# A decoder step's head: small loads issued from GpSimd, bias rows emptied by VectorE, x loaded behind the second unit's pages

## What is computed

```python
def compress(rows, w1, b1, w2, b2):            # cached raw K or V rows, blocks of 32 at a stride of 16
    h = b1
    for r in range(CMP_RATIO):
        h = h + jnp.einsum('bngf,fe->bnge', ch[:, r:r + n_cmp], w1[r])
    return jnp.einsum('bnge,ed->bngd', jax.nn.silu(h), w2) + b2
...
    s = s + tbl[t5_bucket(dist_c)].transpose(2, 3, 0, 1)      # relative-position bias on every score
...
def swiglu_half(x, gain, w_gu, w_down):
    g, u = jnp.split(rms_norm(x, gain) @ w_gu, 2, axis=-1)
    return x + 0.5 * ((jax.nn.silu(g) * u) @ w_down)
```

## Time and profile before

| | |
|---|---|
| median of 3 runs | 3188.43 us (3187.55 to 3188.77) |
| the profiled execution | 3181.32 us |
| its span, first to last instruction | 3179.7 us |
| PE busy | 2992.5 us, 94% of the span |
| PE on the chain that ended last | 91% |
| first matmul of the compression | 47.17 us |
| first matmul of the first block | 255.08 us |

### The profile page before, as it was taken

The page is one execution under the profiler, slowest core; times in us unless marked ns, Lnnn a source line. Parts: engine busy times, 40 slices in busy tenths (PEclk is TensorE's granted clock), DMA queues, the critical chain, the costliest instruction groups (busy, mean ns, idle before and its releaser), DMA issues.

```text
span 3179.7 us, 46641 instructions
## 1 busy us (share of the span) xinstructions
PE 2992.5 (94%) x18952; PEld 2815.2 (89%) x18952; DVE 1450.1 (46%) x1776; ACT 974.3 (31%) x1092; POOL 119.9 (4%) x180
## 2 busy tenths in 40 slices
PE   6999999999999999999994767969999999999999
PEld 3788999999999999999983556649999999999999
DVE  2424445334444444565545434354444433444433
ACT  3423332223222333333323111123343322322322
POOL 0000000000000011100000000121000000000000
PEclk9999999999999999999996655569999999999999
DMA  7364554455554555433214440235454445545444
GB/s 186 101 190 121 149 152 146 139 162 157 150 146 137 148 181 204 147 132 113 107 54 130 137 125 20 65 113 153 139 151 145 137 141 158 159 145 152 131 139 139
DMA packets 675398, 437.43 MB, mean 138 GB/s; under 512 B 29133, under 2 KB 664029, under 8 KB 667741
## 3 DMA queue, kind: packets, MB, share of 16 engines
q1 hardware_dynamic: 661026, 421.29, 44.1%
q0 software_dynamic: 1856, 12.87, 1.1%
q10 hardware_dynamic: 12396, 1.61, 0.5%
HBM read 422.33 MB, written 21.65 MB: 140 GB/s over the span
## 4 chain that ended last, share of the span: by engine, by line
PE 91%; SPq 3%; DVE 2%; issue 1%; ACTq 1%; DMA 1%; POOL 1%; ACT 0%; DVEq 0%; POOLq 0%
PE bank L406 21%; PE bank L407 21%; PE bank L408 21%; PE bank L738 4%; PE bank L740 4%; PE bank L739 4%; PE bank L1266 2%; PE bank L666 2%; PE bank L668 2%; PE bank L667 2%; SPq L1344 1%; PE bank L1105 1%; PE bank L1573 1%; PE bank L1567 1%; SPq L1357 1%
## 5 line engine op out<-in xcount | busy, mean ns | idle before, releaser
L406 PE MATMUL bank<-xh,whi 128*128 128x320 f32 x3072 | 951.4, 310 | 20.1 <-POOL xl L1837 20.1
L407 PE MATMUL bank<-xl,whi 128*128 128x320 f32 x3072 | 950.4, 309 | 0.0
L408 PE MATMUL bank<-xh,wlo 128*128 128x320 f32 x3072 | 950.4, 309 | 0.0
L312 DVE TENSOR_TENSOR wlo<-wraw,whi 128x2048 fp32r<-128x2048 f32 (+1 forms) x321 | 649.8, 2025 | 523.6 <-ACT whi L308 522.7
L308 ACT ACTIVATE whi<-wraw 128x2048 fp32r<-128x2048 f32 (+1 forms) x321 | 543.3, 1693 | 716.9 <-PE bank L408 716.9
L406 PEld LDWEIGHTS bank<-xh,whi 128*128 128x128 f32 x3072 | 578.0, 188 | 21.3 <-POOL xl L1837 21.0
L407 PEld LDWEIGHTS bank<-xl,whi 128*128 128x128 f32 x3072 | 578.0, 188 | 0.2 <-issue 0.2
L408 PEld LDWEIGHTS bank<-xh,wlo 128*128 128x128 f32 x3072 | 577.7, 188 | 0.0
L406 PE MATMUL bank<-hh,whi 128*128 128x320 f32 x1408 | 436.2, 310 | 9.2 <-DVE hl L366 9.2
L407 PE MATMUL bank<-hl,whi 128*128 128x320 f32 x1408 | 435.7, 309 | 0.0
L408 PE MATMUL bank<-hh,wlo 128*128 128x320 f32 x1408 | 435.5, 309 | 0.0
(11 more groups left out here) (308 smaller groups left out, 2568.8 us busy)
## 6 DMA issues: line engine op xcount, KB each, us to landing
wraw<-in_w_ffn_gate_up SPq DMA_DIRECT2D x176, 1024.0 KB, 5.4
wraw<-in_w_ffn_down SPq DMA_DIRECT2D x128, 704.0 KB, 4.5
wraw<-in_w_mix SPq DMA_DIRECT2D x52, 1024.0 KB, 4.8
pages<-in_cache_cmp SPq DMA_DIRECT2D x128, 128.0 KB, 2.1
wraw<-in_w_mix_out SPq DMA_DIRECT2D x16, 1024.0 KB, 5.4
kt_s<-in_slc_k SPq DMA_DIRECT2D x64, 128.0 KB, 2.0
s_v<-in_slc_v SPq DMA_DIRECT2D x64, 128.0 KB
o_win_sample<-in_state_win_kv POOLq DMA_DIRECT2D x8, 1008.0 KB, 15.7
```

The lines of the kernel that those rows point to most:

```text
L312: dve.tensor_tensor(wlo[:, a % 2, 0:size], wraw[:, a % RAW, 0:size], whi[:, a % 2, 0:size].bitcast(F32), ALU.subtract).then_inc(s["lo_read ...
L406: pe.matmul(b, whi[:, a % 2, c], h[:, kk, :], start=first, stop=False)
L407: pe.matmul(b, whi[:, a % 2, c], lo_[:, kk, :], start=False, stop=False)
L408: mm = pe.matmul(b, wlo[:, a % 2, c], h[:, kk, :], start=False, stop=end)
```

## The change

POOL issues the 19 small loads, and the bias store behind them. DVE copies the bias rows, out of four banks instead of two. ACT's list begins with onehot, the table and both halves of the first key weights. `onehot` moves to the memory of `kcs`, `vcs` and `xt`, so x is loaded only when the bias rows are done; it is issued behind the second unit's pages, and its tiles are handled in units 2 to 6. ident is issued behind the first unit's pages. The waits for the small loads move to where they are first needed.

```diff
-N_SMALL = 21
+N_SMALL = 19
...
-        onehot = at("onehot", 172.125, [33, C_ALL])
+        onehot = at("onehot", 8.125, [33, C_ALL])
...
-            return range(KT * (u - 1) // 6, KT * u // 6) if 1 <= u <= 6 else range(0)
+            return range(KT * (u - 2) // 5, KT * (u - 1) // 5) if 2 <= u <= 6 else range(0)
...
-            sp.dma_start(ident[:, :], io["c_ident"]).then_inc(s["ld_ident"], 16)
             sp.dma_start(ptab[:, :], ...).then_inc(s["ld_pt"], 16)
-            first_layer(0, 0).then_inc(s["w1_ld0"], 16)
             sp.wait_ge(s["ld_pt"], 16)
-            unit(0)
-            first_layer(0, 1).then_inc(s["w1_ld1"], 16)
-            sp.dma_start(xt[:, :, :], ...).then_inc(s["ld_x"], 16)
-            for u in range(1, UNITS_C):
+            for u in range(UNITS_C):
                 unit(u)
+                if u == 0:
+                    sp.dma_start(ident[:, :], io["c_ident"]).then_inc(s["ld_ident"], 16)
+                if u == 1:
+                    sp.wait_ge(s["b_mm"], NB_ROWS)
+                    sp.dma_start(xt[:, :, :], ...).then_inc(s["ld_x"], 16)
...
# act_cached, before the first x tile; and in unit 1, before the first SiLU
+                        act.wait_ge(s["ld_small"], 16 * N_SMALL)
# dve_cached
+                if u == 2:
+                    dve.wait_ge(s["ld_small"], 16 * N_SMALL)
# pe_cached, before pe_cached_second of unit 0
+                if u == 1:
+                    pe.wait_ge(s["ld_ident"], 16)
+                    pe.wait_ge(s["ld_small"], 16 * N_SMALL)
...
# scalar
+            act.dma_start(onehot[:, :], io["c_onehot"]).then_inc(s["ld_table"], 16)
+            act.dma_start(table[0:32, :], io["rel_bias_table"]).then_inc(s["ld_table"], 16)
+            for half in range(2):
+                act.dma_start(*first_layer(0, half)).then_inc(s[f"w1_ld{half}"], 16)
-            for n, (dst, src) in enumerate(small):
-                act.dma_start(dst, src, allow_slow_non_contiguous=True).then_inc(...)
-            for k in range(NB_ROWS):
-                nk = min(512, C_ALL - 512 * k)
-                act.wait_ge(s["b_mm"], k + 1)
-                act.activation(brow[:, 512 * k:512 * k + nk], bank[k % 2][0:HEADS, 0:nk], ACT.Copy).then_inc(s["b_row"], 1)
-            act.wait_ge(s["b_row"], NB_ROWS)
-            act.dma_start(scr["bias"], brow[:, :]).then_inc(s["b_out"], 16)
-            act.wait_ge(s["ld_small"], 16 * (N_SMALL - 2))
...
# gpsimd, behind its four memsets, ahead of pool_squares
+            for dst, src in small:
+                pool.dma_start(dst, src, allow_slow_non_contiguous=True).then_inc(s["ld_small"], 16)
+            pool.wait_ge(s["b_row"], NB_ROWS)
+            pool.dma_start(scr["bias"], brow[:, :]).then_inc(s["b_out"], 16)
...
# vector
-            dve.wait_ge(s["ld_small"], 16 * (N_SMALL - 2))
-            dve.wait_ge(s["b_mm"], NB_ROWS)
+            for k in range(NB_ROWS):
+                nk = min(512, C_ALL - 512 * k)
+                dve.wait_ge(s["b_mm"], k + 1)
+                dve.tensor_copy(brow[:, 512 * k:512 * k + nk], bank[k % 4][0:HEADS, 0:nk]).then_inc(s["b_row"], 1)
...
# tensor
-                if k >= 2:
-                    pe.wait_ge(s["b_row"], k - 1)
-                pe.matmul(bank[k % 2][0:HEADS, 0:nk], ...)
+                if k >= 4:
+                    pe.wait_ge(s["b_row"], k - 3)
+                pe.matmul(bank[k % 4][0:HEADS, 0:nk], ...)
             pe.wait_ge(s["b_row"], NB_ROWS)
-            pe.wait_ge(s["ld_ident"], 16)
-            pe.wait_ge(s["ld_small"], 16 * (N_SMALL - 2))
```

More of the change, by code:

```diff
@@ L544, in x_tiles, with first_layer @@
         def x_tiles(u):
-            return range(KT * (u - 1) // 6, KT * u // 6) if 1 <= u <= 6 else range(0)
+            return range(KT * (u - 2) // 5, KT * (u - 1) // 5) if 2 <= u <= 6 else range(0)
+        def first_layer(v, half):
+            return (w1raw[:, 4 * half:4 * half + 4].rearrange("p j r e -> p (j r e)"),
+                    io["w_first"][v, :, 2048 * half:2048 * half + 2048])
         def sync_cached(sp):
@@ L556, in unit @@
                                  ).then_inc(s[f"rows_ld{u % 2}"], 16)
-            def first_layer(v, half):
-                return sp.dma_start(w1raw[:, 4 * half:4 * half + 4].rearrange("p j r e -> p (j r e)"),
-                                    io["w_first"][v, :, 2048 * half:2048 * half + 2048])
-            sp.dma_start(ident[:, :], io["c_ident"]).then_inc(s["ld_ident"], 16)
             sp.dma_start(ptab[:, :], io["page_table"].rearrange("b n -> (b n)").unsqueeze(0)).then_inc(s["ld_pt"], 16)
-            first_layer(0, 0).then_inc(s["w1_ld0"], 16)
             sp.wait_ge(s["ld_pt"], 16)
-            unit(0)
-            first_layer(0, 1).then_inc(s["w1_ld1"], 16)
-            sp.dma_start(xt[:, :, :], io["x_t"].rearrange("(k p) t -> p k t", p=P)).then_inc(s["ld_x"], 16)
-            for u in range(1, UNITS_C):
+            for u in range(UNITS_C):
                 unit(u)
+                if u == 0:
+                    sp.dma_start(ident[:, :], io["c_ident"]).then_inc(s["ld_ident"], 16)
+                if u == 1:
+                    sp.wait_ge(s["b_mm"], NB_ROWS)
+                    sp.dma_start(xt[:, :, :], io["x_t"].rearrange("(k p) t -> p k t", p=P)).then_inc(s["ld_x"], 16)
                 if u == 2:
@@ L573, in sync_cached @@
                         sp.wait_ge(s["w1_lo"], 8)
-                        first_layer(1, half).then_inc(s[f"w1_ld{half}"], 16)
+                        sp.dma_start(*first_layer(1, half)).then_inc(s[f"w1_ld{half}"], 16)
         def act_first_layer(act, v, j):
@@ L1900, in _ @@
         def _(act):
[L1901 to L1917, removed]
@@ L1918, in _ @@
-            for n, (dst, src) in enumerate(small):
-                act.dma_start(dst, src, allow_slow_non_contiguous=True).then_inc(s["ld_table" if n < 2 else "ld_small"], 16)
-            assert len(small) == N_SMALL
-            for k in range(NB_ROWS):
-                nk = min(512, C_ALL - 512 * k)
-                act.wait_ge(s["b_mm"], k + 1)
-                act.activation(brow[:, 512 * k:512 * k + nk], bank[k % 2][0:HEADS, 0:nk], ACT.Copy).then_inc(s["b_row"], 1)
-            act.wait_ge(s["b_row"], NB_ROWS)
@@ L1946, in _ @@
             pool.memset(eps_c[:, :], EPS).then_inc(s["consts"], 1)
+            small = [
+                (w2[:, :, :, :].rearrange("p v t d -> p (v t) d"), io["w_cmp2"][0].rearrange("v (t p) d -> p (v t) d", p=P)),
+                (b1c[:, :], io["b_cmp1"][0].rearrange("v (t p) -> p (v t)", p=P)),
+                (b2k[0:64, :], io["b_cmp2"][0, 0].unsqueeze(1)), (b2k[64:128, :], io["b_cmp2"][0, 0].unsqueeze(1)),
+                (b2v[:, :], io["b_cmp2"][0, 1].unsqueeze(0).to_broadcast([64, HD])),
+                (gain1[:, :], io["norm_ffn1"][0].rearrange("(k p) -> p k", p=P)),
+                (gain_mix[:, :], io["norm_mix"][0].rearrange("(k p) -> p k", p=P)),
+                (gain2[:, :], io["norm_ffn2"][0].rearrange("(k p) -> p k", p=P)),
+                (gain_q[:, :], io["q_gain"]),
+                (gain_k[:, :], io["k_norm"][0].rearrange("b g d -> (b g d)").rearrange("(k p) -> p k", p=P)),
+                (gain_att[:, :], io["att_gain"]),
+                (gain_hg[:, :], io["hgrn_out_norm"][0].rearrange("h d -> d h")),
+                (lowb[:, :, :], io["hgrn_lower_bound"].rearrange("l (h p) -> p l h", p=P)),
+                (same_gt[:, :], io["c_same"]), (pair_ones[:, :], io["c_pair"]), (mask_s[:, :], io["c_mask"]),
+                (gsel[:, :], io["c_seq"]), (caus[:, 0:64], io["c_causal"]), (overlap[:, :], io["c_overlap"]),
+            ]
+            assert len(small) == N_SMALL
+            for dst, src in small:
+                pool.dma_start(dst, src, allow_slow_non_contiguous=True).then_inc(s["ld_small"], 16)
+            pool.wait_ge(s["b_row"], NB_ROWS)
+            pool.dma_start(scr["bias"], brow[:, :]).then_inc(s["b_out"], 16)
             pool.sem_inc(s["nsum"], 4)
@@ L1986, in _ @@
                 nk = min(512, C_ALL - 512 * k)
-                if k >= 2:
-                    pe.wait_ge(s["b_row"], k - 1)
-                pe.matmul(bank[k % 2][0:HEADS, 0:nk], table[:, :], onehot[:, 512 * k:512 * k + nk], start=True, stop=True
+                if k >= 4:
+                    pe.wait_ge(s["b_row"], k - 3)
+                pe.matmul(bank[k % 4][0:HEADS, 0:nk], table[:, :], onehot[:, 512 * k:512 * k + nk], start=True, stop=True
                           ).then_inc(s["b_mm"], 1)
             pe.wait_ge(s["b_row"], NB_ROWS)
-            pe.wait_ge(s["ld_ident"], 16)
-            pe.wait_ge(s["ld_small"], 16 * (N_SMALL - 2))
             pe.wait_ge(s["ch_pad"], 2)
```

## The result

The changed kernel takes 3174.29 us (median of six runs, 3170.83 to 3176.82) beside 3187.99 for the kernel before (six runs, 3182.61 to 3193.29): 13.7 us less, a ratio of 0.9957 with a 95% interval of 0.9944 to 0.9970. The forecast was 3173.4. Timed a second time it had 3171.42 us, ratio 0.9952 (0.9937 to 0.9966). Its profiled execution took 3170.83 us, span 3169.0. Two later executions, one of e6 (6833 us) and one of the kernel before in the rounds of e5 to e8 (5881 us), were in a slow state, and the medians and ratios leave them out.

What follows compares the result with a forecast made beforehand. TensorE was taken to bound the kernel, holding 91% of the chain, except in the first slice, where bias rows wait on ScalarE. Starting compression 15.05 us earlier takes the median 3188.4 to 3173.4 us; range 3169 to 3181.

Steps and rivals of the forecast that it cites:

- The pause and the rows: Kernel's head: bias rows start at 8.71 and run 21.43 us without the wait for ACT from 12.8 to 26.32.
- The sum: Rows end 30.14, last copy 0.35, memsets 0.19, splits 1.44: first compression matmul at 32.12 instead of 47.17, 15.05 us earlier.
- onehot's landing: Lets bias rows start; 0.47 us earlier by earlier issue, so start at 8.71, between bounds 6.9 and 16.0.
- two effects of 1.8 us and up to 7.3: At onehot's landing: weights out of the way bring it 1.8 us sooner; POOL's small loads delay it up to 7.3.
- the bound: Upper limit of small loads crowding onehot: first eight loads all ahead of it, 7.3 us lost, time 3180.7 us.
- Pages of the first unit: SP's page loads before the compression: landed at 26.0, needed by ACT at 30.7, cover 4.7 us.
- x behind the second unit's pages: SP issues x until 38.9, landed at 51.1, splits start about 57; hidden if landed before 75.3.
- The waits on the small loads: After unit two, ACT's first SiLU waits for the last small load, landing at T; hidden, cost nothing.
- three values for T: Last small load's landing on POOL's queue: 22 below, 55 taken as the likely worst, 175 above.
- The deadline itself: Before unit three: the last small load may land as late as 74.0; each microsecond beyond costs one.
- Rival 2: After the second unit: POOL's small loads come too late, price T - 74.0, up to 3274 us; chance 0.12.
- Carrying the head's gain to the end: Everything after the compression shifts by the same amount, as PE bounds it there too: 15.05 us off the total.

Runs made afterwards that it cites:

- e6: Changed kernel with GpSimd's small loads held until onehot and the table landed, second half of first-layer weights issued behind the first unit's pages: 3170.9 us, ratio 0.9952.
- e5: Changed kernel with 20 more element-wise loads of 2048 numbers behind the 19 small ones on GpSimd's queue: 3169.6 us, ratio 0.9947.
- e8: Changed kernel with bf16 bias rows as in e7 plus the edit of e6 (small loads held, second weight half behind the pages): 3164.6 us, ratio 0.9930.
- e1: Kernel before with only the emptying of the bias rows moved to VectorE, four banks; small loads stay on ScalarE's queue: 3177.0 us, ratio 0.9959.
- e2: Kernel before with only the 19 small loads moved to GpSimd's queue; ScalarE still empties rows from two banks: 3173.3 us, ratio 0.9955.
- e7: Changed kernel with onehot in bf16 and the table split into three bf16 parts, loaded ahead of onehot; three matmuls a row: 3169.8 us, ratio 0.9948.
- e3: Changed kernel with onehot back on its old memory, x loaded behind the first unit's pages, its tiles in units 1 to 6: 3172.0 us, ratio 0.9959.
- e4: Changed kernel with 60 more element-wise loads of 2048 numbers behind the 19 small ones on GpSimd's queue: 3249.9 us, ratio 1.0196.

## Why the prediction was right

**The pause and the rows.** This is the mechanism, and it held: e1 and e2 show it. 8.71 was forecast for the start, 8.74 measured; the block of 21.4 us held, at the low clock throughout as before. The sum came out 0.3 us too long behind the rows: the splits took 1.29 us in the chain (30.51 to 31.80) instead of 1.44, ACT's halves being long done, and the last copy and the memsets account for the rest. Two readings were loose without harm: 0.85 us for 512 columns is 1.66 ns each, while 18.02 us over 10.34 rows gives 1.70; the sum uses the 18.02 itself.

**onehot's landing.** Right in value by luck of the choice, wrong in its working: I let two effects of 1.8 us and up to 7.3 cancel, and neither is there. e6, without the small loads and the second half of the weights, moves it by 0.1 to 0.4. What the queues had moved by then (q10 is ACT's, q0 POOL's; packets, MB, share of 16 engines), in the changed kernel from 0 to 8.7:

```profile
q10 hardware_dynamic: 160, 1.39, 67.4%
q0 software_dynamic: 28, 0.11, 4.5%
```

The weights were not out of the way behind onehot: onehot is 0.83 of these 1.39 MB, so over half a megabyte of weights went beside it, on the same queue. And the small loads hardly crowd it: POOL had issued the first eight, all three gains among them, by 8.2, but its packets took 4.5% of 8.7 us, 0.4 us, where the bound has 7.3. (These eight have 7,360 runs, not 7,424.)

**Pages of the first unit.** 26.0 forecast, 26.4 measured. One part was mis-sized: the sixteen issues took SP 19.19 us instead of 17.33; no run isolates why. It cost nothing here; e7 shows that the pages are the next bound.

**x behind the second unit's pages.** Issued at 43.7 instead of 38.5, as the next sixteen issues took 19.93 us too, landed 10.5 us later at 54.2, used at 59.8. Hidden. I priced the moved memory at nothing beyond ACT's halves being hidden; e3 puts it at 1.6 us.

**The waits on the small loads.** Of three values for T (22, 55, 175) I took the middle one as the worst likely; 24.1 was measured, beside the lowest. The 10 us in that lowest sum has no row behind it; the last load took 9.4 to land. The Trainium skill's page "DMA: Bandwidth & Descriptors" (Anatomy of one DMA), by which many descriptors can be emitted before their cost shows, is what the trace bears out here: 0.3 ns a run. e4 adds where it ends: after 14,016 runs in twenty loads POOL stands still, and from there the cost is 0.8 to 1.2 ns a run. Whether runs, loads or what has landed by then sets that point is not shown. The deadline itself, 74.0, was right within 0.3 us. The two units took PE 48.4 us (31.80 to 80.19) instead of 47.75, since the clock rose later, and that made up for the earlier start. Rival 2 was a true mechanism with far too little load: it decides from T = 89.0, and the change is at 24.1.

**Carrying the head's gain to the end.** This step was taken as plain shift. Within their noise the medians bear it out: in the nine timings beside the kernel before other than e4's, they differ by 4.0 us less (e7) to 2.2 us more (e3) than the first matmul moved. A single pair of profiles doesn't, for the clock differs from execution to execution. Three stretches of 15 us each, the end of the compression and two in the first SwiGLU block, with PE's granted clock in the third column from the end; the kernel before:

```profile
240.00:255.00 15.00, 7.70 (x66) 6.97 (x64) 5.85 (x6) 7.94 (x8) 0.00 (x0) 0.66 0.24 71
560.00:575.00 15.00, 12.65 (x86) 12.39 (x86) 6.04 (x7) 3.13 (x3) 0.00 (x0) 1.00 0.33 97
1030.00:1045.00 15.00, 12.93 (x89) 12.67 (x88) 5.54 (x7) 2.82 (x3) 0.37 (x1) 1.00 0.39 107
```

and the changed one, each 15 us earlier:

```profile
225.00:240.00 15.00, 7.70 (x78) 6.98 (x77) 7.32 (x9) 7.94 (x8) 0.00 (x0) 0.89 0.24 71
545.00:560.00 15.00, 12.65 (x76) 12.39 (x75) 4.92 (x7) 2.76 (x2) 0.00 (x0) 0.89 0.34 97
1015.00:1030.00 15.00, 12.94 (x78) 12.67 (x77) 5.05 (x6) 2.76 (x2) 0.37 (x1) 0.89 0.35 96
```

PE pauses for some 7 us in the first of these stretches (7.70 busy of 15) and some 2 us in the other two while it changes from one phase to the next. In one execution the clock falls to half for a moment behind the pause and ten matmuls fewer fit (76 against 86), in another it doesn't. Matching the matmuls of both profiles in their order gives the lead at every point: 15.4 us at the first matmul, 14.7 soon after, since the clock rose later; 16.7 behind 240, where the kernel before had the longer drop; 13.6 behind 560 and 1030, where the changed one had its own; and 10.5 behind the mixer, between 1590 and 2150. There the clock is low most of the time, and where it isn't differs too. Eight microseconds from the same point of the work, the kernel before above and the changed one below:

```profile
1990.00:1998.00 8.00, 8.00 (x46) 6.61 (x44) 0.69 (x1) 1.87 (x5) 0.00 (x0) 0.71 0.01 2
...
1977.00:1985.00 8.00, 8.00 (x38) 6.46 (x36) 0.68 (x1) 1.84 (x5) 0.00 (x0) 0.50 0.01 2
```

The second profile of the kernel before had its own drops near 569 and 1037, and the second of the changed kernel had none there. In the mixer the first profile of the kernel before is the shortest of all twelve: its own repeat is 3.3 us longer, the changed kernel 3.0 and 6.8, the experiments 3.2 to 10.2, with e1 (9.9) and e5 (10.2) the longest, which is why their profiled times stand out. So the 4.9 us missing between the first two profiles come from where the clock happened to fall in each execution, and no part of them is shown to belong to the change. Why it falls behind one pause and not behind the same one in the next execution no run here shows.

## What to carry to other kernels

When an engine's list begins with a long run of DMA issues, look at what it is wanted for first: here one engine issuing for 23 us held up another's work that could have started at 9, and moving either the issues or the work cures it. Price a wait that is moved back as T minus a deadline (T being when what it waits for is there), count the deadline from the chain behind it, and test it from both sides with added loads: here they cost nothing below it and one for one beyond it. A gain at the head of this kernel was passed on to the median within some 4 us, but the first two single profiles show 10.5 us of 15.4, so compare where the clock fell before you look for a loss.

## What the runs showed of the hardware that was not expected

- GpSimd's queue took single-element loads at 0.3 ns a run until 14,016 runs (19 loads of 11,968 runs and one of 2,048) had been issued, by 16.5 us; then it halted for 4 to 10 us before each group of up to seven loads of 2,048 (e4, e5).
- During the bias rows PE stayed at the lower clock without a break, for 21 us in fp32 and for 16 in bf16 (39 matmuls with 33x16 weights in 15.96 us, 0.43 for 512 columns). Behind them the first of the dense 128x128 matmuls at the full pace started 4.8 us after the first of all in the changed kernel and 3.4 in the kernel before, but 3.6 and 5.7 in their second profiles, and up to 6.1 in e3: this varies from execution to execution. The granted-clock column shows 1.00 over the rows all the same; the durations tell the level.
- Onehot and the weights behind it on the same queue moved side by side: 1.39 MB by 8.7 us, of which onehot is 0.83.
- ACT's first table load, 1.28 us, came with ACT's first computation, wherever that was (24.39 in the kernel before, 11.95 in the changed one, 31.20 in e1, 30.45 in e3); in e1 and e3 that put it on the path.
